# Router stage of a two-layer hybrid decoder: router logits computed ahead of the transposes, squares summed from the channel-major residual, group choice on unscaled logits, running sums set up in two parts

## The chip, the cores and the metric

One NeuronCore of a Trainium2 chip runs one program. The metric is the device time of that program in microseconds, median of several runs. The engines are named as the profile names them: PE (TensorE, with PEld for its weight loads), DVE (VectorE), ACT (ScalarE), POOL (GpSimd), SP (SyncE, which issues the weight transfers here).

## What is computed

Two layers over 256 tokens of width 1024, all in float32, then a final RMSNorm. Each layer is a token mixer (three kinds of heads that share an input and an output projection) and a mixture of 32 experts in 4 groups. Only the second half of a layer is touched:

```python
x = x + jnp.einsum('btm,md->btd', mix, w_out)
x = x + hierarchical_moe(rms_norm(x, norm_ffn), router_group, router_expert, router_bias, ...)
# in hierarchical_moe, tok = the normed tokens:
group_prob = softmax(tok @ router_group);  group_p, group_idx = lax.top_k(group_prob, 1)
expert_logits = tok @ router_expert + router_bias        # 4 groups x 8
in_group = take_along_axis(expert_logits, group_idx)     # the 8 of the chosen group
top_logit, top_idx = lax.top_k(in_group, 2)
weights = softmax(top_logit) * group_p
```

Each token goes to two experts of one group. The scale of the RMSNorm is one positive number per token, so that the order of the 4 group logits, which have no bias, is the same with and without it.

## The kernel before

**Layout.** The residual lies channel-major in `xT` (128 partitions x 8 channel tiles x 256 tokens). The router's weights `rws` have been multiplied by the norm's gain (L1564), so the logits can be taken straight from `xT` and scaled afterwards by the token's `rstd`.

**End of the mixer.** PE makes the output projection in four PSUM banks (`("wo", n)`, L871). DVE adds each to two channel tiles of `xT` (L1663), and after each add raises `x_mixed`, so that `x_mixed` counts to 4 in a layer.

**Router.** PE transposes `xT` to token-major tiles `("xt", 0..3)`, 16 transposes of 128x128 (L926). ACT squares the two token tiles out of PSUM with a sum over the row (L1292), makes `rstd` with a Ln and an Exp (L1294, L1295), and writes the scaled tokens `xn` (L1299), which are what the experts' gathers read. PE makes the logits of both token tiles (L932), 8 products of 128x40 each, in one bank. DVE scales them and adds the bias (L1670), then takes the best group (`max`, `max_index`, L1678 and L1679, for each token tile, and the equality L1680), the expert logits of that group (L1684, L1685), the two best experts, and at L1695 the mask `pick[:, 0]`, after which it raises `mask_ready`. PE counts the tokens ahead of each one for each expert (`"rank"`, L954 to L957). DVE turns this into `sel` (L1706) and the selection matrix `Psel` of the first four experts (`select`, L1714). PE gathers the tokens of the first round with it (`gather`, L970, 16 products of 128x128).

**Running sums.** The experts' outputs are summed on top of the residual in PSUM banks 0 to 3. `start_sums` (L940 in layer 0, L943 in layer 1) copies `xT` there with products by the identity. Its end frees `xT`, which is then the last slot of the prefetched expert weights (slot "X").

**Experts.** The 32 experts are done in 8 groups of four ("quads"); each quad takes as many rounds as its fullest expert needs (a round holds 32 tokens of each of four experts). A round reads 12 weight slots of 1 MB: gate and up (L1000), down (L1021), and scatters the result into the sums (L1029, L1033). It holds the gather of the next round (L970), too.

**Order of things.** Each engine runs its instructions in the order in which the program writes them, and waits on semaphores. PSUM banks are given out by a table (`psum_plan`); `begin(name)` waits until the bank's former owner has released it. SP issues all weight transfers in one fixed order (L448 for the mixer's, L456 for the experts'), each waiting until its slot has been released. The mixer's weights and then the experts' have 12 ring slots and 10 more; after the load into slot "X" the next one waits for a slot that an expert product has read.

## Time and profile before

| | |
|---|---|
| median of 3 runs | 851.69 us (850.38 to 852.34) |
| the profiled execution | 851.99 us, its span 850.2 us |
| PE, busy | 791.9 us, 93% of the span |
| DVE, busy | 307.3 us, 36% |
| ACT, busy | 201.8 us, 24% |
| mean granted clock of PE | 0.983 |
| bytes read | 247.04 MB, 292 GB/s over the span |

The share of busy time says that PE is the busiest engine by far. It doesn't say that PE is the limit in every stage: the mixers' stages move few bytes, and the experts' stages move nearly all of them. Times inside the span are counted from its first instruction; the time of the run is 1.8 us longer than the span.

### The profile page before, as it was taken

The page shows a single profiled execution, that of the slowest core. Times are in us where ns is not written, and L with a number is a line of the kernel's source. Part 1 is how long each engine was busy: PE and PEld are TensorE (multiplying, and loading weights), DVE is VectorE, ACT ScalarE, POOL GpSimd, SP SyncE. Part 2 cuts the span into 40 slices and gives each one's busy share as a digit, 9 for nine tenths or more (in the row PEclk, how much of TensorE's full clock was granted, in tenths as well). Part 3 has the DMA queues.
Part 4 walks back from the last instruction along what each step waited for, and adds up shares of the span by engine and source line. Part 5 has one row for each costly group of instructions (what it writes and reads, how often), then busy time and mean ns, then how long its engine had stood idle before and what let it go on. Part 6 is the DMA issues. An engine that isn't in the chain of part 4 may idle for free.

```text
span 850.2 us, 16748 instructions
## 1 busy us (share of the span) xinstructions
PE 791.9 (93%) x6640; PEld 557.7 (66%) x6640; DVE 307.3 (36%) x733; ACT 201.8 (24%) x427; POOL 2.8 (0%) x11
## 2 busy tenths in 40 slices
PE   5999989999999997699999999999999999999776
PEld 4877778888765554355578777788787555445423
DVE  2757333564421111011167663437624111111112
ACT  2253541442300010000114444326212000100002
POOL 1000000000000000000000000000000000000000
PEclk9999999999999999799999999999999999999899
DMA  9842344265789999999995331533658999999996
GB/s 358 357 166 72 126 160 150 100 221 225 295 332 420 419 420 421 421 420 422 419 418 227 113 112 50 205 143 108 267 200 336 421 419 421 421 420 420 421 421 254
DMA packets 36217, 249.11 MB, mean 293 GB/s; under 512 B 4016, under 2 KB 4528, under 8 KB 7088
## 3 DMA queue, kind: packets, MB, share of 16 engines
q1 hardware_dynamic: 35712, 247.39, 72.3%
q8 instruction: 50, 0.82, 0.4%
q10 hardware_dynamic: 432, 0.71, 0.2%
q14 instruction: 23, 0.19, 0.1%
HBM read 247.04 MB, written 1.05 MB: 292 GB/s over the span
## 4 chain that ended last, share of the span: by engine, by line
PE 66%; DMA 17%; DVE 9%; ACT 3%; issue 3%; SPq 1%; DVEq 0%; ACTq 0%; POOLq 0%
PE ps L536 13%; PE ps L1000 11%; PE ps L970 6%; DMA work<-e_up 6%; PE ps L871 6%; PE ps L1021 5%; PE ps L706 4%; DMA more_buf<-e_up 3%; DMA ring<-e_up 3%; PE ps L1033 3%; DMA ring<-e_down 3%; PE ps L1029 3%; PE ps L758 2%; PE ps L560 2%; DVE work L1490 2%
## 5 line engine op out<-in xcount | busy, mean ns | idle before, releaser
L536 PE MATMUL ps<-hT,ring 128*128 128x256 f32 x800 | 183.4, 382 | 0.0
L536 PEld LDWEIGHTS ps<-hT,ring 128*128 128x128 f32 x800 | 148.3, 190 | 22.8 <-issue 3.8
L1000 PE MATMUL ps<-ring,hT 128*32 128x256 f32 x1408 | 84.7, 386 | 5.0 <-DMA ring<-e_gate 3.0
L970 PEld LDWEIGHTS ps<-work,xn 128*128 128x128 f32 x640 | 75.6, 197 | 10.3 <-issue 8.2
L970 PE MATMUL ps<-work,xn 128*128 128x128 f32 x640 | 79.4, 284 | 1.9 <-DVE work L1714 1.9
L1000 PEld LDWEIGHTS ps<-ring,hT 128*32 128x32 f32 x1408 | 43.0, 111 | 42.8 <-issue 10.5
L871 PE MATMUL ps<-xn,ring 128*128 128x256 f32 x256 | 57.8, 381 | 0.0
L871 PEld LDWEIGHTS ps<-xn,ring 128*128 128x128 f32 x256 | 48.1, 190 | 7.2 <-issue 0.7
L1714 DVE TENSOR_TENSOR work<-shapes,sel 128x128 f32<-128x128 f32 x40 | 9.9, 289 | 112.1 <-PE ps L1007 111.9
L1731 DVE TENSOR_TENSOR hT<-ps,pars 128x512 f32<-128x512 f32 x40 | 27.7, 692 | 51.2 <-PE ps L970 51.2
L1783 DVE COPY hT<-ps 128x512 f32<-128x512 f32 x18 | 12.4, 692 | 89.2 <-PE ps L1021 89.2
L1315 ACT ACTIVATE work<-ps 128x256 f32<-128x256 f32 x18 | 6.9, 385 | 157.1 <-PE ps L1000 157.1
L1319 ACT ACTIVATE work<-ps 128x256 f32<-128x256 f32 x18 | 6.9, 384 | 156.7 <-PE ps L1014 156.7
L706 PE MATMUL ps<-ring,hT 128*128 128x128 f32 (+1 forms) x256 | 37.5, 303 | 0.0
L1029 PEld LDWEIGHTS ps<-work,hT 128*128 128x128 f32 x144 | 25.1, 189 | 18.8 <-issue 7.5
L1021 PE MATMUL ps<-ring,work 128*32 128x512 f32 x272 | 33.8, 599 | 3.7 <-ACT work L1319 3.3
L706 PEld LDWEIGHTS ps<-ring,hT 128*128 128x128 f32 x256 | 34.4, 191 | 2.7 <-issue 0.8
L1029 PE MATMUL ps<-work,hT 128*128 128x256 f32 x144 | 36.1, 393 | 0.0
L1033 PE MATMUL ps<-hT,work 128*128 128x512 f32 x72 | 35.9, 621 | 0.0
L1000 PE MATMUL ps<-work,hT 128*32 128x256 f32 x416 | 26.8, 401 | 7.2 <-DMA work<-e_up 7.2
L1780 DVE TENSOR_TENSOR work<-work,ps 128x256 f32<-128x256 f32 x18 | 7.6, 421 | 67.0 <-PE ps L1000 67.0
L1577 DVE TENSOR_TENSOR work<-work,ps 128x192 f32<-128x192 f32 (+1 forms) x48 | 16.9, 353 | 33.3 <-PE ps L758 26.2
(296 smaller groups left out, 885.9 us busy)
## 6 DMA issues: line engine op xcount, KB each, us to landing
ring<-e_gate SPq DMA_DIRECT2D x44, 1024.0 KB, 26.2
ring<-e_up SPq DMA_DIRECT2D x36, 1024.0 KB, 14.7
ring<-w_mix SPq DMA_DIRECT2D x34, 1024.0 KB, 9.7
ring<-e_down SPq DMA_DIRECT2D x28, 1024.0 KB, 27.4
work<-e_down SPq DMA_DIRECT2D x24, 1024.0 KB, 18.0
work<-e_gate SPq DMA_DIRECT2D x12, 1024.0 KB, 10.6
work<-e_up SPq DMA_DIRECT2D x12, 1024.0 KB, 28.1
more_buf<-e_down SPq DMA_DIRECT2D x8, 1024.0 KB, 17.2
```

The costliest lines, as they stand in the source:

```text
L536: mm = pe.matmul(bank, slot_w(i)[:, k, ct * P:(ct + 1) * P], hT3[:, k, :], start=(k == 0), stop=(k == KD - 1))
L560: mm = pe.matmul(bank[:, ct * T:(ct + 1) * T], slot_w(0)[:, k, ct * P:(ct + 1) * P], hU[:, k, :], start=(k == 0), stop=(k == KD - 1))
L706: mm = pe.matmul(bank[:, j * n:(j + 1) * n], hT3[:, k, j * P:(j + 1) * P], w[:, k, 0:n], start=(k == 0), stop=(k == KD - 1))
L758: mm = pe.matmul(z[j][0:rows_, i * HD:(i + 1) * HD], XC[half(j), h, 0:rows_], WC[half(j), h, :], start=True, stop=True)
L871: mm = pe.matmul(ps[:, b, i * T:(i + 1) * T], w[:, k, i * P:(i + 1) * P], mixT[:, k, :], start=(k == 0 and i == 0), stop=(k == KD - 1 and ...
L970: mm = pe.matmul(ps[:, 4 + 3 * half_, kk * P:(kk + 1) * P], xn3[:, j, k * P:(k + 1) * P], Psel[:, j, :], start=(j == 0), stop=(j == TT - 1))
L1000: mm = pe.matmul(ps[32 * e:32 * e + 32, 5 + m, 0:DE], hq[:, k, 32 * e:32 * e + 32], w[:, c0:c0 + DE], start=(k == 0), stop=(k == KD - 1), ...
L1021: mm = pe.matmul(ps[32 * e:32 * e + 32, 5 + h, :], hmT[:, f, 32 * e:32 * e + 32], w[:, e * 512:(e + 1) * 512], start=(f == 0), stop=(f == ...
L1029: mm = pe.matmul(ps[:, k // 2, k % 2 * T:(k % 2 + 1) * T], ysb[:, h, k % 4 * P:(k % 4 + 1) * P], PwT[:, 0:T], start=False, stop=False, ski ...
L1033: mm = pe.matmul(ps[:, 2 * j + h, :], PwT[:, j * P:(j + 1) * P], ysb[:, h, :], start=False, stop=False, skip_group_check=True)
L1490: link(dve.scalar_tensor_tensor(out=e[:, dst], in0=bc[:, src], scalar=col, in1=lim, op0=ALU.add, op1=ALU.min))
L1731: TTn(hq[:, half * 4:half * 4 + 4, :], ps[:, 4 + 3 * half, :].rearrange("p (k s) -> p k s", k=4), gq[:, half * 4:half * 4 + 4].unsqueeze(2 ...
```

## The change

On PE, the router's logits come first, each product as soon as its two channel tiles of `xT` are there, in a bank for each token tile. Between the sixth and the seventh product of the second tile stand two products with a column of ones (`"nsum"`), which sum the squares over the channels. The transposes follow, then the half of `start_sums` for banks 2 and 3, then `"rank"`, and then the half for banks 0 and 1, with the release of `xT` behind it.

On ACT, four squares of `xT` as it is (128x512 each) replace the two squares out of PSUM. On DVE, four adds sum the eight channel tiles of squares to one, the group choice is made on the unscaled group logits, and only then `rstd` is waited for and applied to the 32 expert logits. The exponent of the group's softmax takes `rstd` as its scale, in two instructions on ACT in place of one.

```diff
@@ PE @@
-                for half_ in range(2):
-                    pe.wait_ge(x_mixed, upto(l, x_mixed, 2 * half_ + 2))
-                    for j in range(TT):
+                pe.wait_ge(rwg_ready, upto(l, rwg_ready, 1))
+                for j in range(TT):
+                    bank = begin(("logits", j))
+                    for k in range(KD):
+                        if j == 0 and k % 2 == 0:
+                            pe.wait_ge(x_mixed, upto(l, x_mixed, k // 2 + 1))
+                        if j and k == 6:
+
+                            sq_bank = begin("nsum")
+                            pe.wait_ge(x_summed, upto(l, x_summed, 1))
+                            for i in range(TT):
+                                mm = pe.matmul(sq_bank[:, i:i + 1], hT3[:, 0, i * P:(i + 1) * P], ones[:, 0:1], start=True, stop=True)
+                            done(mm, "nsum")
+                        mm = pe.matmul(bank[:, 0:NLOG], xT[:, k, j * P:(j + 1) * P], rw[:, k, :],
+                                       start=(k == 0), stop=(k == KD - 1))
+                    done(mm, ("logits", j))
+                for j in range(TT):
+                    for half_ in range(2):
                         bank = begin(("xt", 2 * j + half_))
...
-                bank = begin("logits")
-                pe.wait_ge(rwg_ready, upto(l, rwg_ready, 1))
-                for j in range(TT):
-                    for k in range(KD):
-                        mm = pe.matmul(bank[:, j * HD:j * HD + NLOG], xT[:, k, j * P:(j + 1) * P], rw[:, k, :],
-                                       start=(k == 0), stop=(k == KD - 1))
-                done(mm, "logits")
-                for b in (1, 2, 3):
-                    pe.wait_ge(free[b], upto(l, free[b], uses[b]))
...
+                for b in (2, 3):
+                    pe.wait_ge(free[b], upto(l, free[b], uses[b]))
                 start_sums(1)
-                pe.wait_ge(free[0], upto(l, free[0], uses[0]))
-                start_sums(0).then_inc(acc_init, 1)
-                pe.wait_ge(acc_init, upto(l, acc_init, 1))
-                pe.sem_inc(mix_freed, 1)
                 bank = begin("rank")
...
                 done(mm, "rank")
+                for b in (0, 1):
+                    pe.wait_ge(free[b], upto(l, free[b], uses[b]))
+                start_sums(0).then_inc(acc_init, 1)
+                pe.wait_ge(acc_init, upto(l, acc_init, 1))
+                pe.sem_inc(mix_freed, 1)
@@ ACT @@
-                    link(act.activation(hT[:, j * D:(j + 1) * D], ps[:, b:b + 2, :].rearrange("p b n -> p (b n)"), ACT.Square,
-                                        accum_out=ss[:, j:j + 1]))
-                link(act.activation(ss[:, 2:4], ss[:, 0:2], ACT.Ln, scale=1.0 / D, bias=epsc[:, :]))
+                for n in range(4):
+                    act.wait_ge(x_mixed, upto(l, x_mixed, n + 1))
+                    act.activation(hT3[:, 2 * n:2 * n + 2, :], xT[:, 2 * n:2 * n + 2, :], ACT.Square).then_inc(x_squared, 1)
+                bank = get("nsum")
+                link(act.activation(ss[:, 2:4], bank[:, 0:TT], ACT.Ln, scale=1.0 / D, bias=epsc[:, :]))
@@ DVE @@
-                dve.wait_ge(rstd_ready, upto(l, rstd_ready, 2))
-                bank = get("logits")
-                for j in range(TT):
-                    link(dve.scalar_tensor_tensor(out=lg[:, j, :], in0=bank[:, j * HD:j * HD + NLOG], scalar=ss[:, 4 + j:5 + j],
-                                                  in1=pv(l, "router_bias", 0, NLOG), op0=ALU.mult, op1=ALU.add))
-                free_("logits")
+                for m in (2, 6):
+                    dve.wait_ge(x_squared, upto(l, x_squared, m // 4 * 2 + 2))
+                    link(TTn(hT3[:, m - 2:m, :], hT3[:, m - 2:m, :], hT3[:, m:m + 2, :], ALU.add))
+                link(TTn(hT3[:, 0:2, :], hT3[:, 0:2, :], hT3[:, 4:6, :], ALU.add))
+                TTn(hT3[:, 0, :], hT3[:, 0, :], hT3[:, 1, :], ALU.add).then_inc(x_summed, 1)
...
                 for j in range(TT):
+                    bank = get(("logits", j))
+                    link(TTn(lg[:, j, 0:8], bank[:, 0:8], pv(l, "router_bias", 0, 8), ALU.add))
                     link(dve.max(rt[:, j, 8:16], lg[:, j, 0:8]))
...
+                dve.wait_ge(rstd_ready, upto(l, rstd_ready, 2))
+                for j in range(TT):
+                    bank = get(("logits", j))
+                    link(dve.scalar_tensor_tensor(out=lg[:, j, 8:NLOG], in0=bank[:, 8:NLOG], scalar=ss[:, 4 + j:5 + j],
+                                                  in1=pv(l, "router_bias", 8, EXPERTS), op0=ALU.mult, op1=ALU.add))
+                    free_(("logits", j))
```

The order of PE's products between the output projection and the gather, in layer 1 (a row is a run of equal products: the line, tiles written and read, the size of the result, how many), before:

```order
L926 MATMUL ps<-shapes,xT 128x128 x16
L932 MATMUL ps<-rws,xT 128x40 x16
L943 MATMUL ps<-shapes,xT 128x128 x16
L954 MATMUL ps<-pick,shapes 128x64
L955 MATMUL ps<-pick,ones 128x64
L957 MATMUL ps<-pick,ones 128x32
```

and in the changed kernel (its lines are numbered anew: L937 the logits, L935 `"nsum"`, L944 the transposes, L952 `start_sums`, L961 to L964 `"rank"`):

```order
L937 MATMUL ps<-rws,xT 128x40 x14
L935 MATMUL ps<-ones,hT 128x1 x2
L937 MATMUL ps<-rws,xT 128x40 x2
L944 MATMUL ps<-shapes,xT 128x128 x16
L952 MATMUL ps<-shapes,xT 128x128 x8
L961 MATMUL ps<-pick,shapes 128x64
L962 MATMUL ps<-pick,ones 128x64
L964 MATMUL ps<-pick,ones 128x32
L952 MATMUL ps<-shapes,xT 128x128 x8
```

The logits went ahead of the transposes, and eight of the 16 products of `start_sums` went behind `"rank"`, between it and the gather.

DVE from the residual's adds to the expert logits of the chosen group, before:

```order
L1663 TENSOR_TENSOR xT<-xT,ps 128x512 x4
L1670 SCALAR_TENSOR_TENSOR lg<-ps,ss,pars 128x40 x2
L1678 MAX rt<-lg 128x8
L1679 MAX_INDEX rtx<-rt,lg 128x8
L1678 MAX rt<-lg 128x8
L1679 MAX_INDEX rtx<-rt,lg 128x8
L1680 TENSOR_TENSOR rt<-shapes,rtx 128x2x4
L1684 TENSOR_TENSOR pick<-lg,rt 128x64
```

and in the changed kernel:

```order
L1682 TENSOR_TENSOR hT<-hT 128x512 x2
L1683 TENSOR_TENSOR hT<-hT 128x512
L1684 TENSOR_TENSOR hT<-hT 128x256
L1691 TENSOR_TENSOR lg<-ps,pars 128x8
L1692 MAX rt<-lg 128x8
L1693 MAX_INDEX rtx<-rt,lg 128x8
L1691 TENSOR_TENSOR lg<-ps,pars 128x8
L1692 MAX rt<-lg 128x8
L1693 MAX_INDEX rtx<-rt,lg 128x8
L1694 TENSOR_TENSOR rt<-shapes,rtx 128x2x4
L1699 SCALAR_TENSOR_TENSOR lg<-ps,ss,pars 128x32 x2
L1704 TENSOR_TENSOR pick<-lg,rt 128x64
```

Four adds stand ahead of the first look at the logits, and the scaling of the expert logits stands behind the group choice.

## Rows read from the trace of the kernel before

**Rows 1.** The page: what the DMA engines moved in 40 slices of the span.

```profile
GB/s 358 357 166 72 126 160 150 100 221 225 295 332 420 419 420 421 421 420 422 419 418 227 113 112 50 205 143 108 267 200 336 421 419 421 421 420 420 421 421 254
```

**Rows 2.** The chain that ended last, expert stages: start us, us, what.

```profile
399.85 26.09 DMA ring<-e_down
...
803.19 27.32 DMA ring<-e_up
```

**Rows 3.** SP's issues of expert weights in layer 1: start us, us, what.

```profile
644.08 0.33 SPq L456 DMA_DIRECT2D xT<-e_down  x1
651.36 1.19 SPq L456 DMA_DIRECT2D more_buf<-e_down  x2
```

**Rows 4.** Windows: PE, PEld, DVE, ACT, POOL busy (x); PEclk, DMA share, GB/s.

```profile
300.00:400.00 100.00, 87.02 (x916) 50.09 (x905) 14.97 (x34) 6.82 (x16) 0.00 (x0) 0.95 1.01 420
...
651.00:652.00 1.00, 1.00 (x28) 0.59 (x20) 0.86 (x5) 0.00 (x0) 0.00 (x0) 1.00 0.00 0
```

**Rows 5.** Timeline, layer 1: start us, us, engine line, tiles, count, [idle before <-releaser].

```profile
634.81 0.69 DVE L1663 TENSOR_TENSOR xT<-xT,ps 128x512 f32<-128x512 f32 x1 [0.24 <-PE ps L871]
634.85 1.73 PEld L926 LDWEIGHTS ps<-shapes,xT 128*128 128x128 f32 x16 [0.67 <-DVEq L1664]
636.54 3.65 PEld L932 LDWEIGHTS ps<-rws,xT 128*128 128x128 f32 x32
...
638.77 0.30 ACT L1294 ACTIVATE ss<-ss,epsc 128x2 f32<-128x2 f32 x1
...
639.34 1.11 ACT L1299 ACTIVATE xn<-ps,ss 128x1024 f32<-128x1024 f32 x1
640.11 3.65 PEld L943 LDWEIGHTS ps<-shapes,xT 128*128 128x128 f32 x32
640.43 0.55 DVE L1670 SCALAR_TENSOR_TENSOR lg<-ps,ss,pars 128x40 f32<-128x40 f32 x2 [4.93 <-PE ps L932]
641.12 0.17 DVE L1678 MAX8 rt<-lg 128x8 f32<-128x8 f32 x1
...
641.61 0.17 DVE L1678 MAX8 rt<-lg 128x8 f32<-128x8 f32 x1
...
642.28 0.26 DVE L1684 TENSOR_TENSOR pick<-lg,rt 128x64 f32<-128x64 f32 x1
...
644.66 0.41 PE L954 MATMUL ps<-pick,shapes 128*128 128x64 f32 x2 [0.70 <-DVEq L1700]
645.12 0.36 PE L957 MATMUL ps<-pick,ones 128*128 128x32 f32 x2
646.41 3.84 PE L970 MATMUL ps<-work,xn 128*128 128x128 f32 x32 [0.93 <-DVE work L1714]
650.18 1.93 PE L1000 MATMUL ps<-more_buf,hT 128*32 128x256 f32 x32
```

**Rows 6.** Groups by line and shape: xcount | busy us, mean ns | idle before.

```profile
L1127 ACT ACTIVATE work<-work 128x512 f32<-128x512 f32 x6 | 3.3, 619 | 0.1
...
L1548 DVE TENSOR_TENSOR work<-work 128x512 f32<-128x512 f32 x2 | 1.4, 692 | 0.1
L1394 DVE TENSOR_TENSOR xn<-xn 128x512 f32<-128x512 f32 x2 | 1.6, 809 | 0.1
L1395 DVE TENSOR_TENSOR xn<-xn 128x256 f32<-128x256 f32 x2 | 0.8, 424 | 0.1
```

**Rows 7.** Layer 0, timeline and windows around its first gather.

```profile
223.88 3.68 PE L940 MATMUL ps<-xT,shapes 128*128 128x512 f32 x8
228.40 0.41 PE L954 MATMUL ps<-pick,shapes 128*128 128x64 f32 x2 [0.83 <-DVEq L1700]
230.16 5.47 PE L970 MATMUL ps<-work,xn 128*128 128x128 f32 x32 [0.94 <-DVE work L1714]
235.56 1.93 PE L1000 MATMUL ps<-more_buf,hT 128*32 128x256 f32 x32
...
231.50:232.00 0.50, 0.50 (x4) 0.50 (x4) 0.45 (x2) 0.16 (x1) 0.00 (x0) 0.50 1.16 459
```

More of the change, by code:

```diff
@@ L162, in psum_plan @@
     late += [(("wo", 0), 0), (("o", 7), 5), (("on", 5), 4), (("wo", 1), 1), (("on", 6), 6), (("on", 7), 7)]
-    late += [(("xt", 0), 4), (("xt", 2), 6), (("xt", 1), 5), (("xt", 3), 7), ("logits", 0), ("rank", 5)]
+    late += [(("logits", 0), 0), (("logits", 1), 1), ("nsum", 3)]
+    late += [(("xt", 0), 4), (("xt", 1), 5), (("xt", 2), 6), (("xt", 3), 7), ("rank", 5)]
     return front + inv + late
@@ L367, in trunk @@
         x_mixed = sem("x_mixed", 4)
+        x_squared = sem("x_squared", 4)
+        x_summed = sem("x_summed", 1)
         rwg_ready = sem("rwg_ready", 1)
@@ L1286, in _ @@
                 out_rr(7, mrr[:, 2, :])
-                for j in range(TT):
-                    get(("xt", 2 * j))
-                    get(("xt", 2 * j + 1))
-                    b = bank_of[("xt", 2 * j)][0]
-                    link(act.activation(hT[:, j * D:(j + 1) * D], ps[:, b:b + 2, :].rearrange("p b n -> p (b n)"), ACT.Square,
-                                        accum_out=ss[:, j:j + 1]))
-                link(act.activation(ss[:, 2:4], ss[:, 0:2], ACT.Ln, scale=1.0 / D, bias=epsc[:, :]))
+                for n in range(4):
[3 more added lines that the diff above has]
+                link(act.activation(ss[:, 2:4], bank[:, 0:TT], ACT.Ln, scale=1.0 / D, bias=epsc[:, :]))
+                act.sem_inc(free[bank_of["nsum"][0]], 1)
                 act.activation(ss[:, 4:6], ss[:, 2:4], ACT.Exp, scale=-0.5).then_inc(rstd_ready, 1)
@@ L1297, in _ @@
                 for j in range(TT):
+                    get(("xt", 2 * j + 1))
                     b = bank_of[("xt", 2 * j)][0]
@@ L1304, in _ @@
                 act.wait_ge(route_in, upto(l, route_in, 1))
-                act.activation(rt[:, :, 24:28], rt[:, :, 20:24], ACT.Exp).then_inc(route_exp, 1)
+                act.activation(rt[:, 0, 24:28], rt[:, 0, 20:24], ACT.Exp, scale=ss[:, 4:5])
+                act.activation(rt[:, 1, 24:28], rt[:, 1, 20:24], ACT.Exp, scale=ss[:, 5:6]).then_inc(route_exp, 1)
                 act.wait_ge(route_in, upto(l, route_in, 2))
@@ L1665, in _ @@
                     free_(("wo", n))
-                dve.wait_ge(rstd_ready, upto(l, rstd_ready, 2))
-                bank = get("logits")
-                for j in range(TT):
-                    link(dve.scalar_tensor_tensor(out=lg[:, j, :], in0=bank[:, j * HD:j * HD + NLOG], scalar=ss[:, 4 + j:5 + j],
-                                                  in1=pv(l, "router_bias", 0, NLOG), op0=ALU.mult, op1=ALU.add))
-                free_("logits")
+                for m in (2, 6):
[3 more added lines that the diff above has]
+                TTn(hT3[:, 0, :], hT3[:, 0, :], hT3[:, 1, :], ALU.add).then_inc(x_summed, 1)
                 def spread(col, shape):
```

## Prediction

> **What bounds the kernel now.** I read the page's 40 slices first. Two stretches move data at about 420 GB/s without a break, slices 13 to 21 and 32 to 39, the last in part; these are the experts' stages. The mixers' stages in between move less [rows 1]. The chain of waits comes second: it is a chain of PE work, but in each expert stage it passes through transfers of 26 to 28 us that PE had to wait for (one row of each layer is shown) [rows 2]. The windows say the same: from 300 to 400 us the DMA engines were busy all the time at 420 GB/s, and PE 87% [rows 4]. So an expert stage, once its stream of weights runs, ends when the stream ends. What sets the end is the moment at which the stream restarts.
>
> The third view is the list of SP's issues. In layer 1 the load into `xT` was issued at 644.08, and the next one at 651.36, when the first expert products had read a slot [rows 3]; those products began at 650.18 [rows 5]. Between 651 and 652 us nothing was moved at all [rows 4]. The restart therefore hangs on the start of L1000, and every microsecond by which L1000 starts earlier should bring the end of the layer one microsecond forward. Both layers have this shape. The router lies on the path, though PE waits there less than two microseconds.
>
> The fourth view is the timeline of the router in layer 1, in which the clock stayed at its full level. PE is busy from 634.85 on with transposes, logits and `start_sums`; then it waits 0.70 for the mask and, behind `"rank"`, 0.93 for `Psel`. The gather begins at 646.41 and L1000 3.77 later [rows 5]. Ahead of the mask DVE is the long part: from the logits (640.43) to the rank product (644.66) it takes 4.23 us.
>
> **The change part by part, on layer 1's times.** *PE, logits.* 16 products took 640.11 - 636.54 = 3.57 us, 0.223 each; 16 transposes 1.69; 16 products of `start_sums` 3.85 (640.11 to 643.96, which is the 644.66 of the rank less the idle 0.70 before it), so 1.92 for a half [rows 5]. The first product can start at 634.85 as the transposes did: `x_mixed` stands at 3 by then, and the fourth add ends at 635.50 [rows 5], before the seventh product needs it. 14 products end at 634.85 + 3.12 = 637.97.
>
> *The squares.* ACT has 0.62 for a square of 128x512 [rows 6] against 0.93 from one add to the next, so only the last counts: 635.55 + 0.62 = 636.17. DVE's first add fits beside it (635.55 to 636.24). Then come two adds of 128x512 at 0.69 and one of 128x256 at 0.42 [rows 6], with 0.04 between them: 636.28, 637.01, 637.74, end 638.16. With 0.17 for the semaphore, PE passes the wait at 638.33, having stood 0.36. The two products with one column are not in this trace. From below they cost nothing, from above what two logits products cost (same weight loads), 0.45; I take 0.44, since it's the load of a 128x128 tile and not the columns that sets the pace of such products. Two logits products more: 639.22. DVE saw the logits 0.32 after PE went on to its next group (640.11 and 640.43) [rows 5], so now at 639.54, 0.9 earlier than before.
>
> *DVE, group choice.* The first token tile's choice is made while PE is still at the second's. For the second: an add of 128x8, 0.21 with its gap (the 0.17 of a max on eight columns), then `max`, `max_index` and the equality. In the trace both tiles and the equality took 642.28 - 641.12 = 1.16, and one tile 0.49, which leaves 0.67 [rows 5]. That gives 640.42. `rstd` is ready by then: the sums of squares leave PE at 638.8, and from the Ln to the scaling of tokens it was 0.57 (638.77 to 639.34) [rows 5]. The scaling took 0.69 (640.43 to 641.12), and one more release of a bank 0.1: 641.22 for the next instruction, which stood at 642.28. **The mask comes 1.06 earlier**; the rest of DVE's chain to it is unchanged, and the rank product starts at 643.60.
>
> *PE ahead of the rank.* 639.22 + 1.69 + 1.92 = 642.83. PE has then nothing to do for 0.8 us, so DVE decides.
>
> *PE behind the rank.* This is what the change adds to the path. Three rank products take 0.69 (644.66 to 645.12 for two), and then the second half of `start_sums`, 1.92, stands ahead of the gather: 643.60 + 0.69 + 1.92 = 646.21, or 646.16 with the weight load running ahead. Before, from rank to gather, 1.75 passed (644.66 to 646.41), 0.93 of it waiting [rows 5]. DVE's selection now lies beside `start_sums` and costs nothing; if that cover were gone it would cost the 0.93 again. So of the 1.06 the path gives 0.8 back, and **the gather starts 0.25 earlier**. Layer 0 has four products of 128x512 for `start_sums`, 3.68 in total [rows 7], and the same waits; the same 0.25. In sum 0.5 us. ACT's token scaling (two of 1.1 us) starts once the transposes are through, near 640.3, and is done before 643, far ahead of the gather; the second exponent costs 0.2 on an idle ACT.
>
> Bounds for a layer: if DVE's adds take 0.81, as the other row of this shape has it [rows 6], three of them are 0.36 later and the gather is 0.1 later than before. If DVE were not the limit at all, the gather would start at 642.83 + 0.69 + 1.92 = 645.44, 0.97 earlier. So -0.1 to +1.0 a layer, and I stay near the low end because every link of the long way is priced from a row of its own.
>
> *The release of `xT`.* Its load goes out at about 646.2 in place of 644.08. Such a load is 1 MB, 2.5 us at the full rate, and has landed before the restart's data begin (652). It costs nothing as long as it's over by then; if not, it costs what it overlaps, under 1 us.
>
> **The clock.** In layer 0 the same gather took 5.47 and L1000 began 5.40 after it, where layer 1 shows 3.77: 1.63 more. The granted clock was 0.50 there (1.2 GHz in place of 2.4 GHz), and ahead of it PE had stood idle 0.83 and 0.94 within three microseconds [rows 7]. Layer 1 had 0.70 and 0.93 and kept its clock [rows 5]. After the change the second gap is filled by `start_sums`, and what stays (0.36 and 0.8) lies five microseconds apart. I take it that the fall doesn't come: **1.63 less in layer 0**.
>
> The Trainium skill (TensorE: Matmul & The Clock Gate, "Part 1: The HAM clock gate") says that the activity window is free-running, so that the same kernel can find itself in another phase of it from run to run. The two layers agree, one with a fall and one without on the same work. By that rule the profiled fall is one draw, and the changed kernel can draw one too; this is the first rival below.
>
> **The sum.** 851.99 (the profiled execution, span 850.2) - 2 x 0.25 - 1.63 = 849.86. The profiled execution is 0.3 above the median of 851.69, within the spread of the three runs, whose lowest, 850.38, is just 1.6 lower, as if it had no fall. I predict 849.9. A measurement tells this kernel from no change by about 0.2%, 1.7 us: below 849.99 is faster, above 853.4 slower. The forecast lies on that bound.
>
> **The rivals.**
> *A fall stays.* The gap of 0.8 ahead of the rank does what the two gaps did. 851.99 - 0.5 = 851.5. For it: one fall in two layers now. Against it: PE's gaps are shorter and apart. 15%.
> *DVE isn't the limit.* Ops overlap better than their rows say; the gather starts up to 1.0 earlier in each layer: 851.99 - 1.63 - 1.5 = 848.9, at most 848.4. 12%.
> *The adds are late.* Each 0.1 us by which `x_summed` comes late moves logits, mask, rank and gather alike, and no cover is left. At 0.36 late: 851.99 - 1.63 + 0.2 = 850.6. 7%.
> *Hidden anyway.* If the stream were full through the router, nothing would move: 851.7. Against it stands the empty microsecond before the restart [rows 4]. 4%.
> *Slower: the clock falls over the new order.* Logits, one-column products and the wait between them now form one block of 4.4 us (634.85 to 639.22). If that brings the clock down, PE's work from the transposes to the gather's end runs at the lower level, in both layers, and all of it is on the path. A fall costs about 1.63 as in layer 0; two would give 853.1, three 854.7. From three over the two layers on, the kernel is slower. Against it: the 3.57 us of logits in layer 1 were followed by a gather at full pace [rows 5]. 10%.
>
> **How the numbers follow.** The likeliest case, 0.25 a layer and no fall, has 52%; its own spread is 849.2 to 850.6, and 31 of the 52 lie under 849.99, since the median of before may hold more of the fall than I count. Faster: 31 + 12 = 43%. Same: 21 + 15 + 7 + 4 = 47%. Slower 10%. The range goes from the second rival's low end, 848.4, past the case in which a fall stays, to 852.0; beyond it is the last rival and little of the others.
>
> **What would show it.** In the profile after: the first logits product right behind the output projection; PE idle some 0.4 before the one-column products and 0.5 to 1 before the rank; no idle time between rank and gather, with half of `start_sums` there; from the first logits product to the gather 11.3 us, where 634.85 to 646.41 was 11.56; clock 1.00 over both first gathers, and L1000 3.8 behind each. SP's issue behind the load into `xT` moves by as much as L1000 does, and the end of each layer with it. I am wrong if PE stands idle over a microsecond at `x_summed`, if the clock is 0.50 anywhere from the logits to the first round, or if L1000 moves and the last transfer does not.

## The result and the profile after

The changed kernel is slower: 857.66 us (median of 7 runs, 854.52 to 862.73) where the kernel before took 851.69 (7 runs, 850.38 to 852.84); the ratio is 1.0072, its 95% interval 1.0044 to 1.0101. The forecast was 849.9, in a range of 848.4 to 852.0. The profiled execution has a span of 855.0 and a mean clock of 0.978, where before's has 850.2 and 0.983.

The page of the changed kernel: its span, the clock in 40 slices, and what the DMA engines moved, which answers to [rows 1].

```profile
span 855.0 us, 16784 instructions
...
PEclk9999999999999999799999999999999999999898
GB/s 359 352 181 73 117 152 146 99 248 195 295 376 419 419 420 419 422 422 421 418 418 158 124 99 50 210 136 121 269 199 311 424 420 421 420 420 420 421 421 237
```

The expert stages still stream at 420 GB/s. SP's issues in layer 1 answer to [rows 3], the chain of waits to [rows 2].

```profile
649.17 0.33 SPq L459 DMA_DIRECT2D xT<-e_down  x1
654.52 1.79 SPq L459 DMA_DIRECT2D more_buf<-e_down  x2
```

```profile
399.08 26.05 DMA ring<-e_down
...
807.19 27.30 DMA ring<-e_up
834.53 1.93 PE ps L1012 x16
836.46 4.47 PE ps L982 x32
```

The restart of the stream follows the first expert product by 1.18 us (653.34 in the timeline below, 654.52 here), as it did before (650.18 and 651.36 in [rows 3, 5]). The last line is new: the gather behind the last transfer that PE waited for took 4.47 us, where the first ones take 3.83 and the same one took 3.77 in before.

The timeline of the router in layer 1 answers to [rows 5] (start us, us, engine, line, tiles, count, idle before and releaser).

```profile
637.52 3.29 PE L937 MATMUL ps<-rws,xT 128*128 128x40 f32 x28 [0.30 <-DVEq L1677]
...
641.14 0.58 PE L935 MATMUL ps<-ones,hT 128*128 128x1 f32 x4 [0.33 <-DVE hT L1684]
641.58 0.62 PE L937 MATMUL ps<-rws,xT 128*128 128x40 f32 x4
642.02 1.94 PE L944 MATMUL ps<-shapes,xT 128*128 128x128 f32 x16
...
643.80 1.95 PE L952 MATMUL ps<-shapes,xT 128*128 128x128 f32 x16
...
646.36 0.41 PE L961 MATMUL ps<-pick,shapes 128*128 128x64 f32 x2 [0.60 <-DVEq L1720]
...
647.02 2.03 PE L952 MATMUL ps<-shapes,xT 128*128 128x128 f32 x16
649.58 3.83 PE L982 MATMUL ps<-work,xn 128*128 128x128 f32 x32 [0.53 <-PE ps L952]
653.34 1.93 PE L1012 MATMUL ps<-more_buf,hT 128*32 128x256 f32 x32
```

The rank product (L961) comes 8.84 us after the first logits product, where 9.78 passed before. The gather (L982) comes after 12.06, where it was 11.53: ahead of it stands an idle 0.53 whose releaser is PE itself, L952. In layer 0, windows and timeline show the other half of the matter, and answer to [rows 7] (columns of a window: PE, PEld, DVE, ACT, POOL busy, PEclk, DMA share, GB/s).

```profile
222.66 2.88 PE L944 MATMUL ps<-shapes,xT 128*128 128x128 f32 x16
225.33 2.67 PE L949 MATMUL ps<-xT,shapes 128*128 128x512 f32 x4
...
230.90 3.83 PE L982 MATMUL ps<-work,xn 128*128 128x128 f32 x32 [0.52 <-PE ps L949]
```

```profile
223.50:227.00 3.50, 3.50 (x14) 2.52 (x12) 2.72 (x16) 2.23 (x2) 0.00 (x0) 0.51 1.03 433
493.00:496.50 3.50, 3.44 (x12) 2.74 (x11) 2.70 (x6) 0.00 (x0) 0.00 (x0) 0.52 0.00 0
541.00:544.50 3.50, 3.50 (x19) 3.50 (x18) 0.00 (x0) 0.98 (x2) 0.00 (x0) 0.52 0.94 393
834.50:838.00 3.50, 3.47 (x24) 2.20 (x25) 0.42 (x1) 0.00 (x0) 0.00 (x0) 0.51 1.01 414
```

The gather of layer 0 has its full pace (5.47 before), but the clock is at 0.51, near 1.2 GHz, over the transposes and `start_sums` just behind the new block: 2.88 for what layer 1 does in 1.94. It is also low in two places of layer 1's mixer, where before has none, and behind the last transfer that PE waited for.

The span falls into stages by four marks of the timeline. *Router* is from the first PE product behind the output projection to the first expert product; *experts* from there to the next mixer, or to PE's last product; *mixer 1* from there to the router's first product. All are in us.

```
                   router 0  router 1  experts 0  mixer 1  experts 1   span
before                16.94     15.30     194.13   205.19     194.28  850.2
before_again          15.31     15.30     194.45   206.84     194.24  850.6
after                 16.51     15.82     194.22   208.63     195.94  855.0
after_again           17.82     17.86     194.91   207.51     195.06  858.1
```

Before_again and after_again are the same kernels once more, from the first experiments. The loss lies in three places: the routers, the mixer of layer 1, and the last expert stage. In the first pair of traces the mixer carries most of it (3.44 of 4.8 us) and the routers almost nothing (0.1 together); in the second pair the routers carry 5.1 of 7.5. So no single trace gives the shares.

### The profile page after: what moved, and what is told of

Same layout as the page of the kernel before. It is cut to its first block, busy times and chain, and to the rows that moved or that the text cites. A ratio compares the mean times of both kernels' runs of the same rounds, so it can differ in the third digit from the quotient of the medians.

```text
span 855.0 us, 16784 instructions
## 1 busy us (share of the span) xinstructions
PE 796.9 (93%) x6648; PEld 560.5 (66%) x6648; DVE 312.8 (37%) x745; ACT 202.6 (24%) x429; POOL 2.8 (0%) x11
## 4 chain that ended last, share of the span: by engine, by line
PE 67%; DMA 17%; DVE 8%; ACT 3%; issue 3%; SPq 1%; DVEq 0%; ACTq 0%; POOLq 0%
PE ps L539 14%; PE ps L1012 11%; PE ps L982 6%; DMA work<-e_up 6%; PE ps L874 6%; PE ps L1033 5%; PE ps L709 4%; DMA more_buf<-e_up 3%; DMA ring<-e_up 3%; PE ps L1045 3%; DMA ring<-e_down 3%; PE ps L1041 3%; PE ps L761 2%; PE ps L563 2%; DVE work L1503 2%
## 5 line engine op out<-in xcount | busy, mean ns | idle before, releaser
L982 PEld LDWEIGHTS ps<-work,xn 128*128 128x128 f32 x640 | 73.7, 193 | 9.9 <-issue 9.9
L982 PE MATMUL ps<-work,xn 128*128 128x128 f32 x640 | 77.5, 280 | 1.0 <-PE ps L952 0.5
```

Source lines behind the costliest of these rows:

```text
L982: mm = pe.matmul(ps[:, 4 + 3 * half_, kk * P:(kk + 1) * P], xn3[:, j, k * P:(k + 1) * P], Psel[:, j, :], start=(j == 0), stop=(j == TT - 1))
```

## Experiments

Each kernel ran beside the kernel before on the same chip. That one had medians of 852.51, 852.63, 852.32 and 852.93 in the four jobs, of 15 to 23 runs each.

**1 and 2. Both kernels once more (before_again, after_again),** without an edit.

> The kernel before once more, for a second trace. Theory A (placing): the half-clock stretches come at fixed steps of time, and a build meets them at about the same places every time, so that this trace shows none in layer 1's mixer (450 to 640 us) again, as the first one did; times 850.4 to 852.9. Theory B (chance): the steps start anywhere in each execution; this trace then has its half-clock stretches shifted against the expert stages by any amount, and runs of this kernel should sometimes lie 3 us and more above 852.8. Theory C (router): the lost time lies between the residual's adds and the first expert product; this trace shows 15.3 us there in layer 1 (start of the products that follow the output projection to the first expert product) and nothing else changes.

> The changed kernel once more, for a second trace. Theory A: half-clock stretches in layer 1's mixer again (about 493 and 541 us in the first trace), 3 us of the loss there; 854 to 859. Theory B: they lie elsewhere or are missing, and the time follows their count. Theory C: 15.8 us in the router of layer 1, all of 5 us or more lost there or in the expert stages and none in the mixer.

Before_again: 852.47 (10 runs), 0.9995 [0.9983, 1.0007]. After_again: 859.48 (4 runs), 1.0080 [1.0063, 1.0096]. In before_again neither first gather had a low clock: 3.84 in each layer. Theory A is out: before_again has a low stretch in layer 1's mixer (539.0 to 542.4) where the first trace of the same kernel has none, and after_again has one (543.0 to 546.4) where after has two. Theory C, that all is lost in the routers and the expert stages, is out too: with that stretch before_again's mixer took 206.84 where before's took 205.19. After_again had a low clock in both routers; the timeline and windows of its layer 1:

```profile
639.43 3.83 PE L937 MATMUL ps<-rws,xT 128*128 128x40 f32 x28 [0.30 <-DVEq L1677]
643.06 0.99 PE L935 MATMUL ps<-ones,hT 128*128 128x1 f32 x4
...
644.77 3.65 PE L944 MATMUL ps<-shapes,xT 128*128 128x128 f32 x16
648.22 2.24 PE L952 MATMUL ps<-shapes,xT 128*128 128x128 f32 x16
...
653.53 3.83 PE L982 MATMUL ps<-work,xn 128*128 128x128 f32 x32 [0.62 <-PE ps L952]
```

```profile
639.00:642.00 3.00, 2.70 (x25) 2.60 (x24) 2.45 (x5) 1.26 (x2) 0.00 (x0) 1.00 1.04 431
642.00:648.00 6.00, 6.00 (x30) 6.00 (x30) 3.66 (x20) 1.58 (x3) 0.00 (x0) 0.50 1.01 425
```

The first logits still have clock 1.00; from 642 on, PE is busy all the time and the clock is 0.50. That is 2.6 us after the first logits product and a microsecond before the one-column products (643.06), with the wait for `x_summed` ahead of them. The gather comes 14.10 after the first product.

**3. The gather's own wait away (after_nodrain).** The semaphore comes with the last product, and PE does not wait for itself.

```diff
-                start_sums(0).then_inc(acc_init, 1)
-                pe.wait_ge(acc_init, upto(l, acc_init, 1))
-                pe.sem_inc(mix_freed, 1)
+                start_sums(0).then_inc(mix_freed, 1)
```

> The changed kernel, but the last product of the second half of start_sums releases xT by itself, in place of PE waiting for that product and releasing it then. The gather should start 0.5 us earlier in each layer (0.53 us of idle time stands between start_sums and gather in the trace). Theory C: 1.0 us faster than the changed kernel, 856.7. Theory A and B: the half-clock stretches meet layer 1 at another place, so the time can move by 1 to 5 us either way, and the trace names the stretches that did it.

857.02 (6 runs), 1.0048 [1.0030, 1.0066], 0.3 from the 856.7 of theory C. The idle 0.53 is gone:

```profile
647.53 2.03 PE L952 MATMUL ps<-shapes,xT 128*128 128x128 f32 x16
649.39 3.74 PE L980 MATMUL ps<-work,xn 128*128 128x128 f32 x32
```

From rank to gather it is 2.45 us, where after has 3.22 and after_again 3.24. The clock was at 0.50 in both routers all the same, so the wait is one cause and not the whole.

**4. Both halves of the sums ahead of the rank, with the wait (after_sums_first).**

```diff
                 start_sums(1)
+                for b in (0, 1):
+                    pe.wait_ge(free[b], upto(l, free[b], uses[b]))
+                start_sums(0).then_inc(acc_init, 1)
+                pe.wait_ge(acc_init, upto(l, acc_init, 1))
+                pe.sem_inc(mix_freed, 1)
                 bank = begin("rank")
...
-                start_sums(0).then_inc(acc_init, 1)
-                pe.wait_ge(acc_init, upto(l, acc_init, 1))
-                pe.sem_inc(mix_freed, 1)
```

> The changed kernel with both halves of start_sums ahead of the rank, as in the kernel before; the early logits, the squares and the group choice on unscaled logits stay. My prediction's arithmetic: PE is done with start_sums at 639.2 + 1.7 + 3.85 = 644.8 on the clock of the trace before, so the rank starts there and the gather 1.75 later, 646.6, against 646.41 before. Theory C: 0.3 to 0.5 us a layer faster than the changed kernel, about 857. Theory A and B: as above, moved by 1 to 5 us either way with the stretches.

858.31 (4 runs), 1.0074 [1.0047, 1.0102], where about 857 was expected. Layer 0 had no fall, and its router took 15.72; layer 1 had one (636.9 to 643.7) and took 18.79. The place of the sums doesn't save the kernel. Between its two layers stand 3.1 us, and what differs is the clock.

**5 and 6. What brings the clock down (before_narrow8, before_wide4).** Both put work of about 1.8 us ahead of before's logits: eight products of 40 columns, or four of 256. Its results are written over.

```diff
+                for k in range(KD):
+                    pe.matmul(bank[:, 0:NLOG], xT[:, k, 0:P], rw[:, k, :], start=(k == 0), stop=(k == KD - 1))
                 for j in range(TT):
```

```diff
+                for k in range(4):
+                    pe.matmul(bank[:, 0:T], c("ident"), xT[:, k, :], start=(k == 0), stop=(k == 3))
                 for j in range(TT):
```

> The kernel before with eight more products of 128x40 ahead of the logits (the first token tile's logits twice, overwritten by the real ones; the output is unchanged). Theory N (the narrow products bring the clock down): the block of 40-column products is 5.35 us long in place of 3.57, so that 1.78 us a layer come directly, and the clock is 0.50 behind the block in both layers, 2.5 us more each: 852.5 + 3.6 + 5 = 861. Rival W (any wait does it, and the narrow products have nothing to do with it; no wait is added here): 852.5 + 3.6 = 856.1, clock full in the router.

> The kernel before with four more products of 128x256 ahead of the logits, of the same time on PE as eight of 128x40 (1.75 us), overwritten by the logits; the output is unchanged. Both theories: 852.5 + 3.5 = 856.0, clock full in the router. It is the control for the narrow ones: if this kernel is also at 861, the clock does not care what the products are, only where they stand.

860.37 (4 runs, one of them at 926.48), 1.0098 [1.0078, 1.0119], and 860.34 (4 runs), 1.0099 [1.0082, 1.0116]. The first is what the theory of narrow products expected (861), the second is 4 us above it (856). So the time alone doesn't tell the theories apart; the traces do. Layer 1 of before_narrow8, timeline and window:

```profile
639.01 1.88 PE L931 MATMUL ps<-rws,xT 128*128 128x40 f32 x16
640.71 4.76 PE L934 MATMUL ps<-rws,xT 128*128 128x40 f32 x32
645.28 6.08 PE L945 MATMUL ps<-shapes,xT 128*128 128x128 f32 x32
```

```profile
643.00:650.00 7.00, 7.00 (x36) 7.00 (x35) 3.56 (x21) 1.11 (x1) 0.00 (x0) 0.52 0.80 339
```

And of before_wide4:

```profile
642.10 3.66 PE L934 MATMUL ps<-rws,xT 128*128 128x40 f32 x32
645.59 3.82 PE L945 MATMUL ps<-shapes,xT 128*128 128x128 f32 x32
651.85 5.47 PE L972 MATMUL ps<-work,xn 128*128 128x128 f32 x32 [0.93 <-DVE work L1716]
```

```profile
645.00:651.50 6.50, 5.23 (x45) 4.96 (x44) 4.14 (x24) 0.89 (x3) 0.00 (x0) 1.00 0.90 347
652.00:655.00 3.00, 3.00 (x15) 3.00 (x16) 1.24 (x6) 1.28 (x1) 0.00 (x0) 0.50 0.58 238
```

Behind the lengthened block of 40-column products the clock is low for 6.8 us in both layers, with no idle time ahead of it. Behind the same logits with wide products before them it stays up. It then falls in the gathers of both layers, behind the idle times of before, which is the fall that before's layer 0 shows in [rows 7]. So there are two kinds of place, and the theory that narrow products bring the clock down has its support from the first. The two falls in the gathers, which neither theory had, are most of the 4 us by which the second kernel missed its forecast.

**7 and 8. The block cut, or its wait moved (interleaved, nsum_later),** both without PE's own wait. The first puts the transposes of a token tile right behind that tile's logits; the second keeps 16 logits in one block and sends the one-column products behind the first four transposes.

```diff
                     done(mm, ("logits", j))
-                for j in range(TT):
                     for half_ in range(2):
```

```diff
-                        if j and k == 6:
...
+                        if j == 0 and half_ == 0:
+                            sq_bank = begin("nsum")
+                            pe.wait_ge(x_summed, upto(l, x_summed, 1))
```

> The changed kernel with the transposes of the first token tile between the two tiles' logits (the order is logits 0, transposes 0, logits 1 with the sum of squares, transposes 1), and without PE's wait for the end of start_sums. The block of narrow products is cut in two pieces of 1.8 and 2.2 us, and the wait for x_summed disappears, since 0.9 us of transposes come before it. Theory N: no stretch of 0.50 in the router; the second tile's logits come 0.4 us later than in the changed kernel, the gather 11.7 us after PE's start (before: 11.56): 852 to 853, 5 us faster than the changed kernel. Theory B of the first batch (the half-clock stretches fall by chance): as the changed kernel without the wait, 857.

> The changed kernel with the two one-column products behind the first four transposes, so that the 16 logits products run without a wait in one block of 3.57 us as long as in the kernel before, and without PE's wait for the end of start_sums. If the wait for x_summed and the one-column products inside the block bring the clock down, it stays up here: gather 10.7 us after PE's start in place of 11.56, 0.8 a layer earlier, 851.0. If it is enough that the narrow block follows the 0.30 us of idle time behind the output projection, where the kernel before had the transposes in between, the stretches of 0.50 stay: 855 to 857.

854.16 (7 runs), 1.0032 [1.0019, 1.0045], and 854.32 (10 runs, 850.82 to 856.47), 1.0021 [1.0005, 1.0036]. Neither trace has a low clock in a router, and the routers take 15.30 and 15.36, 14.54 and 14.61. The forecasts, 852 to 853, and 851.0 or 855 to 857, were missed by 1.2 and 0.7 us or more. Both are slower than before, though their routers aren't: mixer 1 took 207.4 in both (206.84 in before_again, which has a low stretch there as well), and the last experts 195.64 and 196.55. Interleaved differs from after_nodrain in the order of the transposes alone: no low clock in two routers against one in both, and 1.0032 [1.0019, 1.0045] against 1.0048 [1.0030, 1.0066], which overlap.

**9. The place of later instructions (before_moved).** The changed kernel has 17 more instructions in DVE's stream and 5 more in ACT's by the end of layer 0's router. This kernel is before with as many waits on a semaphore that was met long ago, none of them on the path.

```diff
+                if l == 0:
+                    for _ in range(17):
+                        dve.wait_ge(init_done, 6)
```

> The kernel before with 17 waits on DVE and 5 on ACT added in layer 0, ahead of its expert loops, on a semaphore that has long been reached; they stand where both engines wait anyway and compute nothing. They put every DVE and ACT instruction of layer 1 as many places later in the program as the changed kernel does. Theory D (place in the instruction stream): the changed kernels show gaps of 0.37 us on DVE and ACT in layer 1's mixer that no semaphore explains (first one 18.9 us after the mixer's start), which the kernel before doesn't have at these instructions; they come from the places and not from the router. Then this kernel has the same gaps, its mixer of layer 1 is 0.65 us longer, and the median is 0.7 to 2 us above the kernel before, 853.3 to 854.5. Rival (the router's new order causes them): no gaps there, 852.5.

853.51 (12 runs), 1.0014 [1.0004, 1.0025]: 1.2 us slower (0.3 to 2.1 by the interval), inside the 853.3 to 854.5 expected. Its mixer 1 took 207.17, where before_again and before_filled, with a low stretch at the same place, took 206.84 and 206.83: 0.34 longer and not the 0.65 expected. So the time came as forecast, and its trace shows only part of it. One row of layer 1's mixer, in before, in the changed kernel, and in this one:

```profile
448.57 0.21 DVE L1425 TENSOR_TENSOR gz<-ps,pars 128x48 f32<-128x48 f32 x1 [0.25 <-DVE xn L1372]
```

```profile
448.15 0.21 DVE L1438 TENSOR_TENSOR gz<-ps,pars 128x48 f32<-128x48 f32 x1 [0.62 <-DVE xn L1385]
```

```profile
448.02 0.21 DVE L1428 TENSOR_TENSOR gz<-ps,pars 128x48 f32<-128x48 f32 x1 [0.62 <-DVE xn L1375]
```

The releaser is the same and the wait 0.37 longer, with no other change to that work.

**10 and 11. 32 places, and three quarters of the sums ahead (nsum_later_realigned, three_quarters).** The first is nsum_later with 15 waits more on DVE and 27 on ACT, which with the change's own 17 and 5 makes 32 each. The second is that with only the last bank of `start_sums` left behind the rank:

```diff
                 start_sums(1)
+                pe.wait_ge(free[0], upto(l, free[0], uses[0]))
+                start_sums(0, [0])
                 bank = begin("rank")
...
+                pe.wait_ge(free[1], upto(l, free[1], uses[1]))
+                start_sums(0, [1]).then_inc(mix_freed, 1)
```

> The kernel nsum_later with 15 waits more on DVE and 27 on ACT in layer 0, at the same place. With the change's 17 and 5 that makes 32 each. The gaps in the traces stand 32 instructions or a multiple of it apart, so 32 places later should have them where the kernel before has them. Theory D: mixer of layer 1 0.65 us shorter than in nsum_later, router 14.6 us in both layers as there, median 0.7 us or more below 854.3. If the period isn't 32, the mixer has its gaps at some third set of places.

> The kernel nsum_later_realigned with three of the four banks of start_sums ahead of the rank in place of two. In nsum_later PE stands idle 0.72 to 0.79 us there and has 1.9 us of start_sums behind the rank; 0.93 is what DVE needs from the rank to the gather. The rank comes 0.2 later, the gather 0.5 to 0.6 earlier: 14.0 us from PE's start to the first expert product, 1.1 us less over both layers than nsum_later_realigned, if the clock stays full.

855.39 (5 runs), 1.0037 [1.0024, 1.0050], and 853.29 (12 runs, 847.5 to 855.85), 1.0015 [0.9999, 1.0031]. The gap went back to 0.25 in the first:

```profile
446.01 0.21 DVE L1438 TENSOR_TENSOR gz<-ps,pars 128x48 f32<-128x48 f32 x1 [0.25 <-DVE xn L1385]
```

But layer 1's router had a low clock (636.8 to 643.7) and took 16.93, and the kernel is no faster than nsum_later, where under 853.6 was expected. Its mixer 1 did get shorter, 206.38 for 207.40, with one low stretch in each. In the trace of three_quarters the routers took 13.95 and 13.93, the shortest of all, with a span of 845.4; ten of its twelve runs lie between 852.8 and 855.9 and two near 847.6. The 1.1 us expected over both layers came (27.88 for the 29.15 of nsum_later, both at full clock), but the trace is of one of the two short runs. Of the other ten only the mean granted clock is on record: 0.972 to 0.976, where the two have 0.984 and 0.986. They had more low clock, and where it lay isn't known.

**12. Everything together, with the block cut (interleaved_three):** interleaved, with the three quarters and the 32 places of the runs before.

> The kernel interleaved (transposes of the first tile between the two tiles' logits) with three of the four banks of start_sums ahead of the rank and with the 15 and 27 waits that put layer 1 of DVE and ACT 32 places later. PE stood idle 1.5 us ahead of the rank in interleaved, so one bank more there is free; the gather should be bound by DVE's selection, 10.9 us after PE's start, and the first expert product 14.7 (before: 15.3). Theory N (narrow products in one block bring the clock down): clock full in the router in all runs, 1.2 us faster than the kernel before, 851.1, and no runs at 855 and more. Rival (nothing about the router's order matters, and half of the runs of any changed kernel are 3 us slower by the places where the half-clock stretches fall): 853 to 854 like three_quarters.

**850.44 (6 runs, 849.58 to 850.90), 0.9971 [0.9959, 0.9982]: 0.3% faster than the kernel before, and faster than the changed one.** Layer 1:

```profile
632.85 1.95 PE L937 MATMUL ps<-rws,xT 128*128 128x40 f32 x16 [0.30 <-DVEq L1678]
634.62 1.07 PE L943 MATMUL ps<-shapes,xT 128*128 128x128 f32 x8
635.53 1.43 PE L937 MATMUL ps<-rws,xT 128*128 128x40 f32 x12
...
638.59 2.84 PE L951 MATMUL ps<-shapes,xT 128*128 128x128 f32 x24
642.02 0.41 PE L962 MATMUL ps<-pick,shapes 128*128 128x64 f32 x2 [0.58 <-DVEq L1721]
642.68 1.14 PE L951 MATMUL ps<-shapes,xT 128*128 128x128 f32 x8
643.77 3.84 PE L980 MATMUL ps<-work,xn 128*128 128x128 f32 x32
```

```profile
632.00:640.00 8.00, 7.70 (x68) 7.33 (x67) 5.79 (x19) 3.84 (x7) 0.00 (x0) 1.00 0.98 412
```

The gather comes 10.92 after the first product and the first expert product 14.69, in both layers, at full clock. The mean clock was 0.980 to 0.984 in all six runs. The time is 0.7 under the 851.1 expected. Only 1.2 of the 2.5 us gained over the kernel beside it are the routers' (14.69 for 15.30 in each layer); its mixer 1 took 204.83, without a low stretch, so part of the gain is that of the places.

**13 and 14. The places alone, and the gap alone (after_realigned, before_filled).** The first is the changed kernel with the 15 and 27 waits. The second is before with the last bank of the sums behind the rank and without PE's own wait, which fills the gap ahead of the gather and leaves all else.

> The changed kernel itself with nothing but the 15 and 27 waits in layer 0. Theory D: gaps in layer 1's mixer as in the kernel before, 0.7 to 2 us less than the changed kernel: 856.0 to 857.5. What stays is the router's part, 0.5 us a layer from the wait for start_sums and some 2.5 us for each half-clock stretch. If theory D carried most of the loss, it would be at 853.

> The kernel before with the last quarter of start_sums (bank 1) behind the rank in place of ahead of it, and without PE's wait for the end of start_sums; logits, squares and transposes as before. It is my prediction's term for the clock by itself: the second of the two gaps (0.93 us ahead of the gather) is filled with work, and the gather starts no later, since DVE needs these 0.93 anyway. As predicted then: no clock 0.50 in the first gathers, 1.63 us less for each layer that had it (one of four in the two traces of the kernel before), so 0.5 to 1.6 us less: 850.7 to 851.8. Rival: the gap ahead of the rank is 0.96 longer for it (1.7 in one piece) and brings the clock down in its stead: 852.3 or more.

855.73 (8 runs), 1.0040 [1.0023, 1.0057], and 852.88 (11 runs), 1.0000 [0.9992, 1.0009]. In after_realigned mixer 1 took 204.83, but the clock was low in both routers, which took 17.65 and 16.63. Before_filled starts its gather as before, 11.5 after the first product, without idle time, and is as fast as before: the 850.7 to 851.8 expected of it, from what is left of the clock term, was a miss. The rival's 852.3 or more fits the time but not the trace, in which the gap of 1.59 ahead of the rank is there and no router has a low clock. After_realigned came 0.3 under its 856 to 857.5.

The count over all traces, of routers with a stretch at half clock: of the changed order's block with the wait in it (after, after_again, after_nodrain, after_sums_first, after_realigned) 8 of 10; of the uncut block without the wait 1 of 6; of the cut block 0 of 4; of before's order (before, before_again, before_moved, before_filled) 1 of 8, and that one at the gather. A trace is one execution, so these counts are few, and three_quarters' is of one of its two short runs. Of the 8 falls, 6 begin 2.6 to 3.2 us after the first logits product, ahead of the wait and the one-column products (3.6 after it), and the other 2 begin 5.3 after it, behind them. The one of the uncut block without the wait begins 3.3 after it.

## Why the prediction was wrong

**The bound held.** Experts 0 takes 193.8 to 194.9 us in every trace, and the restart follows the first expert product by 1.18 us. What moves the router moves the restart, and with it the end, as far as the stage behind the restart keeps its length.

**The working up to the rank held.** It forecast 8.75 us to the rank product and 1.06 saved; it was 8.84 and 0.94. The wait at the one-column products was 0.33 (0.36 forecast), their cost 0.44 (0.44), the wait ahead of the rank 0.60 (0.8).

**The step "PE behind the rank" failed.** It forecast 2.56 from rank to gather (643.60 to 646.16) and "no idle time between rank and gather"; it was 3.22 (646.36 to 649.58). The diff puts `acc_init`'s wait directly ahead of the gather, where PE waits for the end of its own last product, 0.53 us. Before, the same wait stood ahead of the rank, under DVE's chain, and so cost nothing. With it the way to the gather is 0.53 longer at full clock (12.06 against 11.53 in layer 1) where 0.25 less was forecast. That is 2 x 0.78 = 1.6 us of the miss of 7.8 (857.66 for 849.9). After_nodrain shows the idle time go: its 2.45 from rank to gather behind the 8.84 up to the rank makes 11.29, the 11.3 that was forecast. So this wait is the term that the sum left out.

**The clock term, 1.63, was the second step that failed.** "I take it that the fall doesn't come: 1.63 less in layer 0" was right of the gather, whose clock was full in both layers. But the median of before didn't hold the fall: before_again has none in either gather, and filling the gap alone is worth nothing (before_filled, 1.0000). The Trainium skill (TensorE: Matmul & The Clock Gate, "Part 1: The HAM clock gate") has the window free-running, so that the same kernel can meet it in another phase. The two traces of before agree in part: the stretch at 231.3 is in the first alone and those at 122.6, 324.0 and 539.0 in the second alone, while the ones near 348, 798 and 825 are in both. A term read from one draw of such a thing should have been weighed by how often it comes: one of the six gathers in before, before_again and before_moved had it.

**The last rival, given 10%, is what happened, though not as it was told.** In the five traces with the changed order's block the clock falls to 1.2 GHz in 8 of 10 routers. It isn't the block as a whole that does it, with its wait and its one-column products: 6 of the 8 falls begin ahead of these, while PE is at the first 14 logits products. And the low stretch is over before the gather, whose clock was full each time. Over the three traces with the kernel's own router order (after, after_again, after_realigned) the router takes 17.05 on average, over four of before's order 15.5 (both layers; 15.30 without the fall): 1.5 a layer, 3.1 us in all. The gather's extra 0.53 stands in this at full clock too, so about 1.0 a layer is the clock. The argument against the rival was that 3.57 us of logits had kept the clock in layer 1; those stood behind the transposes. Before_narrow8 shows that eight more such products are enough, in both layers and even behind the transposes. The short wait is not needed: the falls ahead of it show that, and so does before_narrow8. Without it 1 of 6 routers fell all the same, against 8 of 10; up to the wait PE runs the same products in both kinds, so this difference can be chance, and if it isn't, its cause is open. Length alone isn't it either: the falls begin within 3.3 us of narrow products, where before's 3.57 behind the transposes had none in eight routers. What the place behind the output projection adds, no run takes apart.

**What no term counted.** The instructions added to DVE and ACT, semaphore instructions among them, move all that follows. Before_moved shows 1.2 us for that alone [0.3 to 2.1]. The mixer of layer 1 gives a size by itself. In the traces without a low stretch there it took 205.2 in before and before_narrow8, 205.87 in after_nodrain and after_sums_first, with the change's places, and 204.8 in after_realigned, three_quarters and interleaved_three, with 32. One low stretch adds 1.6 (206.8 in before_again, before_filled and before_wide4). So of the 3.4 that mixer 1 lost in after's trace some 0.7 are the places and the rest its two low stretches. Such stretches are in 4 of the 6 traces in before's order and in 5 of the 10 others, so that nothing shows that the change brings them. After_realigned is at 1.0040 [1.0023, 1.0057] where the changed kernel is at 1.0072 [1.0044, 1.0101] and 1.0080 [1.0063, 1.0096]; the first pair overlaps, so what the places cost the changed kernel, 2.7 to 3.4 us by these ratios, is an estimate, and more than the mixer shows.

The last expert stage is 0.8 to 1.7 longer in the changed kernel's traces. Behind the last transfer that PE waited for the clock is low in before's traces too, for 1.3 to 1.6 us, and leaves the gather there at 3.77; in after it is low for 3.4 and takes in the gather (the 4.47 above), which is 0.85 of the 1.7. In after_again what follows that transfer is as long as in before. The rest, 0.7 to 0.8 in both, lies ahead of that transfer's end and stays open; no run took that stage apart.

**What the range missed.** Its upper end, 852.0, came from a case in which one known fall stays. The case that new falls come had its price, 854.7, and stood outside. It was excluded on one row of one layer, and even its price lacked the wait of 0.53, the places and the last stage.

## What to carry to other kernels

A wait of an engine for its own completion is free only under another engine's chain: when work is moved behind what it used to hide under, move the wait with it in the sum, and hang the semaphore on the last product instead where the order of products already protects the data. Try products of few columns mixed with wide ones before you gather them in one block: interleaved_three (0.9971 [0.9959, 0.9982]) differs from three_quarters (1.0015 [0.9999, 1.0031]) in the cut and in the place of the one-column products alone, and the clock fell in 0 of 4 cut routers and in 9 of 16 uncut ones. That holds of this kernel; why it does is open. Don't take a fall of the clock that one profile shows as part of the median before a second profile of the same kernel shows it at the same place.

## What the runs showed of the hardware

The granted clock fell while PE was busy without a break: in layer 1 of before_narrow8 PE was busy for 3.20 of the 3.20 us from 640.0 to 643.2 with clock 1.00, all of it products of 128x40, and then for all of the 6.80 with clock 0.50. In after_again it fell 2.6 us into the logits, with PE busy for 2.00 of the last 2.00 us. That is not the fall behind idle time that before's layer 0 and before_wide4 show.

A wait of PE for its own last product, with nothing beside it, stood at 0.52 to 0.62 us (after, after_again).

DVE had a gap 0.37 us longer at one fixed place of its stream, which 17 added instructions brought and 32 took away again. No row names its cause.
